# A quarter of the second tokens' expert products on GpSimd and ScalarE, value sums in PSUM, a second tile read early

## What is computed

```python
def chunk(zc):                      # 128 tokens at a time
    ...
    expert = jnp.take_along_axis(cand_idx, top_pos, axis=-1)
    gate = jax.nn.softmax(top_s, axis=-1)
    u = jnp.take(peer_u, expert, axis=0)
    act = jax.nn.gelu(jnp.einsum('chkd,cd->chk', u, zc))
    v = jnp.take(peer_v, expert, axis=0)
    w = (gate * act.astype(jnp.float32)).astype(zc.dtype)
    return jnp.einsum('chk,chkd->cd', w, v).astype(zc.dtype)
...
return rmsnorm_2(h, norm_f_g)
```

## Time and profile before

| | us |
|---|---|
| runs before (3) | 2689.12, 2693.78, 2695.74; median 2693.78 |
| profiled execution, its own time | 2692.59 |
| its span in the trace | 2690.8 |
| gather of both tables up to the last product | about 1453 to 2239 |
| pause | about 2242 to 2300 |
| dense stage | about 2300 to 2679 |

### The profile page before, as it was taken

The page is one execution under the profiler, slowest core; times in us unless marked ns, Lnnn a source line. Parts: engine busy times, 40 slices in busy tenths (PEclk is TensorE's granted clock), DMA queues, the critical chain, the costliest instruction groups (busy, mean ns, idle before and its releaser), DMA issues.

```text
span 2690.8 us, 32133 instructions
## 1 busy us (share of the span) xinstructions
PE 2288.9 (85%) x11532; PEld 1824.2 (68%) x11532; DVE 2130.7 (79%) x3227; ACT 1024.4 (38%) x1517; POOL 636.3 (24%) x706
## 2 busy tenths in 40 slices
PE   8999989999999999989899955545656558999998
PEld 7997778888888888879788831111223225777776
DVE  6986647665666566577766999899999998999997
ACT  5433554443444344454542111000234334544443
POOL 1000000000000000000002354433444442577772
PEclk9999999999999999999999975666677777999999
DMA  6533345555555555544658999999999995999996
GB/s 225 186 122 106 121 145 172 187 187 187 188 187 187 187 186 177 181 128 141 203 179 360 421 419 419 420 419 419 417 411 405 407 413 212 339 388 392 391 395 235
DMA packets 314375, 730.99 MB, mean 272 GB/s; under 512 B 21025, under 2 KB 223009, under 8 KB 275745
## 3 DMA queue, kind: packets, MB, share of 16 engines
q0 software_dynamic: 73728, 402.69, 37.0%
q1 hardware_dynamic: 240402, 325.99, 35.9%
q10 hardware_dynamic: 144, 1.05, 0.1%
HBM read 727.57 MB, written 2.10 MB: 271 GB/s over the span
## 4 chain that ended last, share of the span: by engine, by line
DVE 29%; PE 15%; DMA 8%; issue 5%; POOL 1%; ACT 1%; DVEq 0%; PEldq 0%; ACTq 0%; SPq 0%; POOLq 0%
DVE row L2483 13%; DMA row<-in_peer_u,expert 7%; DVE acc L2494 6%; PE pl L849 4%; PE pl L856 3%; PE pg L1278 2%; DVE spread_lo L2633 2%; DVE hot_b L2520 1%; PE pl L852 1%; PE pl L853 1%; PE pl L1243 1%; DMA row<-in_peer_v_rows,expert 1%; PE pl L1172 1%; POOL row L787 1%; PE pl L1269 1%
## 5 line engine op out<-in xcount | busy, mean ns | idle before, releaser
L1936 DVE TENSOR_TENSOR wlo<-raw,whi 128x1024 fp32r<-128x1024 f32 (+1 forms) x436 | 517.8, 1208 | 374.9 <-ACT whi L1335 373.1
L1243 PE MATMUL pl<-row,diag 128*128 128x512 f32 x452 | 347.0, 913 | 307.2 <-DMA row<-in_peer_v_rows,expert 268.9
L2483 DVE CUSTOM_DVE_ANT_0 row<-row,pg 128x2048 f32<-128x2048 f32 x256 | 574.4, 2283 | 35.5 <-DMA row<-in_peer_u,expert 34.5
L1335 ACT ACTIVATE whi<-raw 128x1024 fp32r<-128x1024 f32 (+1 forms) x436 | 444.1, 1038 | 412.6 <-PE pl L856 407.8
L849 PE MATMUL pl<-x_split,whi 128*128 128x512 f32 x1888 | 478.5, 395 | 10.3 <-DVE x_split L1944 5.4
L1243 PEld LDWEIGHTS pl<-row,diag 128*128 128x128 f32 x452 | 110.4, 269 | 499.6 <-issue 424.1
L787 POOL DMA_INDIRECT row<-in_peer_v_rows,expert x256 | 364.9, 1425 | 248.7 <-DVE acc L2494 88.5
L849 PEld LDWEIGHTS pl<-x_split,whi 128*128 128x128 f32 x1888 | 341.6, 190 | 74.5 <-issue 7.5
L856 PE MATMUL pl<-x_split,wlo 128*128 128x256 f32 x2656 | 373.7, 284 | 3.9 <-DVE wlo L1936 3.9
L856 PEld LDWEIGHTS pl<-x_split,wlo 128*128 128x128 f32 x2656 | 359.0, 192 | 23.1 <-DVE wlo L1936 4.5
L787 POOL DMA_INDIRECT row<-in_peer_u,expert x256 | 240.2, 938 | 364.6 <-DVE dots L2483 187.0
(11 more groups left out here) (345 smaller groups left out, 2876.3 us busy)
## 6 DMA issues: line engine op xcount, KB each, us to landing
v_tile<-in_peer_v_dense SPq DMA_DIRECT2D x128, 512.0 KB, 5.9
raw<-in_w_in SPq DMA_DIRECT2D x51, 1024.0 KB, 5.2
raw<-in_w_gate SPq DMA_DIRECT2D x44, 1024.0 KB, 5.1
raw<-in_w_up SPq DMA_DIRECT2D x44, 1024.0 KB, 5.1
raw<-in_w_out SPq DMA_DIRECT2D x32, 1024.0 KB, 5.7
raw<-in_w_down SPq DMA_DIRECT2D x32, 1024.0 KB, 5.7
wq<-in_peer_wq SPq DMA_DIRECT2D x15, 1024.0 KB, 11.7
raw<-in_w_down SPq DMA_DIRECT2D x16, 768.0 KB, 4.8
```

Source lines behind the costliest of these rows:

```text
L1243: last = mm(pl_all[:, c:c + width], diag[:, (at - 1) % 4, :], row[b][:, c - DENSE:c - DENSE + width], start=at == 1, stop=at == ADDED_ROWS ...
L1335: return nc.scalar.activation(o, i, ACT.Copy)
L1936: V.tensor_tensor(wlo[:, n % 4, 0:k, :], w[:, :, f, :], whi[:, n % 4, 0:k, :].bitcast(F32), ALU.subtract)\
L2483: V.tensor_tensor_reduce(row[b][:], row[b][:], z_tok[:], 1.0, 0.0, ALU.mult, ALU.add, dots[:, at:at + 1])\
```

## The change

- In the second tokens the products with k % 4 == 1, 32 of 128, have the user "split": GpSimd multiplies the row in place with `z_copy`, a copy of z in SBUF (VectorE writes it once, in the place of `gain_d`), after issuing the row six entries later; ScalarE sums it into `dots` ahead of the entry three later. The buffer is free after ScalarE's sum.
- One value row more is added by TensorE (114).
- Sums of value rows go to PSUM: those of the first tokens onto TensorE's sum in pl[2] and pl[3], those of the second tokens into pl[0] and pl[1], and are added to `acc` once a token set. The groups of the pause use pg[0] to pg[2].
- The second tile has a home of its own and is read in the pause (`m == 2`).
- The gains are spread in four steps at tiles 100, 102, 106 and 108, and ScalarE copies them to SBUF.

Lines that only name semaphores or stand unchanged are left out:

```diff
@@ -62,7 +62,7 @@
 DENSE = 1024
 GATHERED = D - DENSE
 EARLY = 100
-ADDED_ROWS = 113
+ADDED_ROWS = 114
...
 def row_user(table, t, n, k):
 
     if table == "u":
-        return "dot"
+        return "split" if t and k % 4 == 1 else "dot"
...
-GAIN_AT = 64
+SHARED = PH * TOPK // 4
+
+
+def dots_by(heads):
+
+    return [sum(row_user("u", *divmod(n, PH), k) == user for n in range(heads) for k in range(TOPK)) for user in ("dot", "split")]
+
+
+def shared_row(j, after):
+
+
+    return [r for r, what in enumerate(ROW_ORDER) if row_user(*what) == "split" and min(r + after, LATER + 3) == j]
+
+
+GAIN_AT = 80
+GAIN_TILES = (100, 102, 106, 108)
...
+        z_copy = sb("z_copy", "arena", TT * D + 2 * PH * NKEY, [P, D])
...
-        tile_homes = [("arena", 2 * D), ("arena", 4 * D), ("arena", 4 * D + DENSE),
-                      ("rest", choice_at), ("rest", choice_at + DENSE)]
-        high_homes = [("arena", 2 * D + DENSE), ("arena", 3 * D + DENSE), ("rest", choice_at + 2 * DENSE)]
+        tile_homes = [("arena", 2 * D), ("arena", 3 * D + DENSE), ("arena", 4 * D), ("arena", 4 * D + DENSE),
+                      ("rest", choice_at)]
+        high_homes = [("arena", 2 * D + DENSE), ("rest", choice_at + DENSE), ("rest", choice_at + 2 * DENSE)]
...
+        gain_all = sb("gain_all", "raw", 3 * D, [P, D])
...
-        used_by = {"dot": dot_done, "add": row_added, "sum": row_summed}
+        shared_done, SHARED_DONE = lam_exp, 1
+        shared_ready, SHARED_READY = sq_added, 6 * len(ADDED)
+        used_by = {"split": shared_done, "dot": dot_done, "add": row_added, "sum": row_summed}
...
-            sp.wait_ge(dot_done, PRODUCTS)
+            sp.wait_ge(dot_done, PRODUCTS - SHARED)
+            sp.wait_ge(shared_done, SHARED_DONE + SHARED)
             sp.wait_ge(row_added, EARLY)
             for m in range(NKEY):
-                if m == 1:
+                if m == 2:
...
+            def shared_product(r):
+
+                b, use, count, _ = ROW_PLAN[r]
+                if count == 1:
+                    pool.wait_ge(z_ready, 3)
+                pool.wait_ge(row_full[b], 16 * use)
+                nc.gpsimd.tensor_tensor(row[b][:], row[b][:], z_copy[:], ALU.mult).then_inc(shared_ready, 1)
...
+                if j == LATER + 4:
+                    pool.wait_ge(shared_ready, SHARED_READY + SHARED)
...
-                    pool.wait_ge(used_by[user], count)
+                    pool.wait_ge(used_by[user], count + (SHARED_DONE if user == "split" else 0))
                 at = t * HROWS + n * TOPK + k
                 dst, rows = (row[b][:], A["peer_u_2"][0]) if table == "u" else (row[b][:, 0:GATHERED], A["peer_v_rows"])
                 nc.gpsimd.indirect_dma_start(dst, None, rows, bass.IndirectOffsetOnAxis(ap=expert[:, at:at + 1], axis=0))\
                     .then_inc(row_full[b], 16)
+                for r in shared_row(j, 6):
+                    shared_product(r)
...
-                banks = [pl[0], pl[1], pg[0]] if t else [pl[0], pl[1]]
+                banks = pg[0:3] if t else pl[0:2]
...
-            def gain_rows():
+            def gain_rows(q):
 
                 pe.wait_ge(gain_in, 16)
                 pe.wait_ge(sums_ready, 1)
-                for q in range(4):
-                    last = mm(pl[q], ones[0:1, :], gain_row[0:1, q * 512:(q + 1) * 512], start=True, stop=True)
-                last.then_inc(gain_ready, 1)
+                if q >= 2:
+                    pe.wait_ge(gain_copied, 1 + q - 1)
+                mm(pl[2 + q % 2], ones[0:1, :], gain_row[0:1, q * 512:(q + 1) * 512], start=True, stop=True).then_inc(gain_ready, 1)
 
 
             pe.wait_ge(sc_ready, 2 * PH)
@@ -1321,8 +1352,8 @@
             pe.wait_ge(spread_ready, TT * GROUPS)
             for m in range(NKEY):
                 dense(m)
-                if m == NKEY - 16:
-                    gain_rows()
+                if m in GAIN_TILES:
+                    gain_rows(GAIN_TILES.index(m))
...
-                act.wait_ge(dot_done, (pair + 1) * 2 * TOPK)
+                done, shared = dots_by(2 * pair + 2)
+                act.wait_ge(dot_done, done)
+                if shared:
+                    act.wait_ge(shared_done, SHARED_DONE + shared)
...
-                bank = [pl[0], pl[1], pg[0]][g % 3] if t else pl[g % 2]
+                bank = pg[g % 3] if t else pl[g % 2]
...
+            def shared_sum(r):
+
+                b, _, count, _ = ROW_PLAN[r]
+                _, t, n, k = ROW_ORDER[r]
+                at = t * HROWS + n * TOPK + k
+                act.wait_ge(shared_ready, SHARED_READY + count)
+                activation(row[b][:], row[b][:], ACT.Copy, accum_out=dots[:, at:at + 1]).then_inc(shared_done, 1)
+
             u = 0
-            for table, t, n, k in ROW_ORDER[:LATER]:
+            for j, (table, t, n, k) in enumerate(ROW_ORDER[:LATER + 4]):
+                for r in shared_row(j, 3):
+                    shared_sum(r)
+                if j >= LATER:
+                    continue
...
+                if m - HIGHS in GAIN_TILES:
+                    q = GAIN_TILES.index(m - HIGHS)
+                    act.wait_ge(gain_ready, q + 1)
+                    copy(gain_all[:, q * 512:(q + 1) * 512], pl[2 + q % 2]).then_inc(gain_copied, 1)
+            act.wait_ge(sums_ready, 2)
             square(1, slice(DENSE, D), 43)
...
+                if t == 0 and at == ADDED_ROWS:
+                    dve.wait_ge(row_added, ADDED_ROWS)
                 if count > 1:
                     dve.wait_ge(row_summed, count - 1)
+                a = pl_all[:, 0:GATHERED] if t else pl_all[:, DENSE:]
+                if (t, n, k) == (1, 0, 0):
+                    V.tensor_scalar(a, row[b][:, 0:GATHERED], dots[:, at:at + 1], None, ALU.mult).then_inc(row_summed, 1)
+                else:
+                    V.scalar_tensor_tensor(a, row[b][:, 0:GATHERED], dots[:, at:at + 1], a, ALU.mult, ALU.add).then_inc(row_summed, 1)
+
+            def add_sums(t):
+
+                dve.wait_ge(row_summed, SUMMED_ROWS if t else HROWS - ADDED_ROWS)
                 a = acc[:, t, DENSE:]
-                V.scalar_tensor_tensor(a, row[b][:, 0:GATHERED], dots[:, at:at + 1], a, ALU.mult, ALU.add).then_inc(row_summed, 1)
-
-            def add_sums():
-
-                dve.wait_ge(row_added, ADDED_ROWS)
-                dve.wait_ge(row_summed, HROWS - ADDED_ROWS)
-                a = acc[:, 0, DENSE:]
-                V.tensor_tensor(a, a, pl_all[:, DENSE:], ALU.add).then_inc(sums_ready, 1)
+                V.tensor_tensor(a, a, pl_all[:, 0:GATHERED] if t else pl_all[:, DENSE:], ALU.add).then_inc(sums_ready, 1)
...
-                dve.wait_ge(gain_ready, 1)
+                dve.wait_ge(gain_copied, 5)
                 dve.wait_ge(fin_rstd, t + 1)
                 for q in range(4):
                     c = slice(q * 512, (q + 1) * 512)
-                    V.scalar_tensor_tensor(acc[:, t, c], acc[:, t, c], small[:, 36 + t:37 + t], pl_all[:, c], ALU.mult, ALU.mult)\
+                    V.scalar_tensor_tensor(acc[:, t, c], acc[:, t, c], small[:, 36 + t:37 + t], gain_all[:, c], ALU.mult, ALU.mult)\
...
+                    V.scalar_tensor_tensor(z_copy[:], acc[:, 1, :], small[:, 57:58], gain_d[:], ALU.mult, ALU.mult)\
+                        .then_inc(z_ready, 1)
                 for k in range(TOPK):
-                    product(t, n, k)
+                    if row_user("u", t, n, k) == "dot":
+                        product(t, n, k)
...
-                        add_sums()
+                        add_sums(0)
                 r = rows_by(m)
-            dve.wait_ge(row_summed, SUMMED_ROWS)
+            add_sums(1)
```

More of the change, by code:

```diff
@@ L395, in build @@
         freq_read = sem("freq_read")
+        gain_copied = freq_read
         par_in = sem("par_in")
@@ L1883, in _ @@
                     square(0, slice(DENSE, D), 41)
-            act.wait_ge(row_summed, SUMMED_ROWS)
+                if m - HIGHS in GAIN_TILES:
[3 more added lines that the diff above has]
+            act.wait_ge(sums_ready, 2)
             square(1, slice(DENSE, D), 43)
```

## The result

The changed kernel takes **2716.6 us** (median of 4 runs, 2714.6 to 2722.5) against 2693.3 before on the same chip: ratio 1.0088, 95% interval 1.0075 to 1.0101. The forecast was 2690 with a range to 2711; the result lies outside it. The profiled execution took 2714.57 us, its span is 2712.7.

The account below looks back on a forecast made before the run. The prediction took transfers and VectorE to stand side by side in the second tokens' gather, with 6.8 us recoverable. Terms -3.4 + 1.7 - 1.3 - 2.5 + 1.8 = -3.7 gave 2688.9, by the median 2690; range 2682 to 2711.

Parts of the forecast that it names:

- VectorE simply ceases to be the pace: Second tokens' gather: with 70.7 us of products removed, VectorE no longer limits; only 6.8 us can come back.
- term of -3.4 us for the gather: Second tokens' gather: half of the 6.8 us comes back, as only six or seven rows stay under way; ends 0 and -6.8.
- Locks between the two: Rival, 8%: in the second tokens' gather GpSimd's multiplies hold VectorE's hot-key groups and selection, 49 us; about 2707.
- 367, which still fits: Under the locks rival, VectorE's work in the second tokens' gather, 386 - 70.7 + 2.4 + 49, against some 394 us.
- Ceiling of the relief, 6.8 us: Second tokens' gather: 300 us at 410 GB/s would take 293.2 at 419.5, the most that sparing VectorE returns.
- The multiply, 4.6 us: Second tokens' gather: GpSimd's 128x2048 multiply takes 4.6 us, kept range 4.3 to 5.2, from a 128x512 add.
- GpSimd's pace as the bound: Rival, 22%: from z to the turn GpSimd's rounds set the time; 2700 to 2712 us, middle 2705.
- This stall is covered: GpSimd's first multiply waits for z_copy until about 1847.9, while eight rows (17 us) are under way.
- 2.3 us of lag is free: End of the gather: the split rows' weights are ready at 2239.7, before TensorE comes at 2242.0.
- The second tile, -2.5: Second tile read in the pause: VectorE waits less before tile 1's split, -2.5 us, ends 0 and -3.5.
- The 14th row, +1.7 and -1.3: One more row added by TensorE lengthens the pause by 1.7 us and takes 1.3 us from the dense stage.
- The sums in PSUM, +1.8: Dense stage: 142 sums each cost 13 ns more in PSUM, +1.8 us; lower end 0, +11 without overlap.

Follow-up runs that it names:

- e1: The changed kernel without the split, all 128 products of the second tokens on VectorE again; 2686.1 us, 0.9982 of the kernel before.
- e4: The changed kernel with the first tokens' hot_b reading key numbers from PSUM in place of SBUF; 2691.4 us, 0.9993 of the kernel before.
- e3: The kernel before with 32 products of the second tokens taken over 64 columns in place of 2048; 2688.8 us, ratio 0.9996.
- e10: The changed kernel without the split and with 113 added rows as before; 0.9986 of the kernel before.
- e6: The changed kernel with hot_b's key numbers in PSUM and the first head's products not split (28 rows split); 2691.2 us, 1.0000 of the kernel before.
- e8: The changed kernel with each GpSimd multiply cut in four of 128x512, no waits between; 2731.5 us, 1.0146 of the kernel before.
- e9: The changed kernel with each GpSimd multiply cut in four pieces, each waiting for the one before; 2712.5 us, 1.0084 of the kernel before.
- e7: The changed kernel without the split, with 32 GpSimd fills of a 128x2048 buffer at the multiplies' places; 2695.7 us, 1.0020 of the kernel before.

## Why the prediction was wrong

In the forecast's own sum the step that failed is "VectorE simply ceases to be the pace", with its term of -3.4 us for the gather. VectorE stayed 98% busy, with 82.5 us of held operations in the place of the products taken off, and the gather became 31.0 us longer. The forecast had this case among its rivals: **it is the rival "Locks between the two"**, at 8% the second smallest. It had the right pair of engines, and its price was too low. It counted 56 places, a chance of 38% and 2.3 us each: 49 us. Measured: 25 meetings of 3.3 us, 82.5 us. A mean over a random start underrates it, since both engines act on the same event: GpSimd comes to its multiply when VectorE frees a buffer, and VectorE's next work after that product is often the group. (That is argued from the timeline, not shown by a run.) The kind of operation was also named too narrowly: the rival speaks of two SBUF inputs, which the gate product has (9.8 of the 82.5 us), while hot_b (53.9), the conversion (15.4) and the shift (3.4) read one tile. Then it set the result against VectorE's whole stretch, "367, which still fits"; with 82.5 us in the place of 49 its own sum gives 400, which doesn't fit into its 394. And the stretch isn't even. Cut at z + 60 us and at turn - 70 us, the middle part reads:

```profile
1903.65:2174.50 270.85, 152.36 (x377) 76.43 (x378) 267.42 (x515) 98.48 (x219) 114.64 (x122) 0.74 1.01 410
```

in e1, and

```profile
1899.99:2200.54 300.55, 160.24 (x383) 79.67 (x384) 294.97 (x475) 143.69 (x267) 217.25 (x149) 0.70 0.95 380
```

in the change: VectorE is 98.7% and 98.1% busy. In e1 the transfers stand beside it at 410 GB/s; in the change they have fallen to 380, and VectorE's work alone is the length. By the groups of these windows it lost 44 us of products (85 to 65) and got 69 more of held operations (hot_b 34.2 to 84.1, conversion 1.1 to 12.3, gate product 0.6 to 8.5): +25 of the +27.6. The other products were spared at the edges, where VectorE waits for rows anyway.

**The reason given against that rival was no evidence.** "No row here shows a VectorE operation held by GpSimd" was true because GpSimd ran nothing but issues in this stretch; it says nothing of what a multiply does. The Trainium skill says in "SBUF — State Buffer", Who interferes with whom, that whichever comes first keeps the shared pair for the whole instruction, and that a conversion or TENSOR_SCALAR between SBUF tiles, and, against a GpSimd instruction that reads SBUF, an operation with two SBUF inputs are kinds that can want it. The kinds agree here: the held ones are these, the products and the reductions are not held, and one operand moved to PSUM ends it (796 to 402 ns). On who comes first the trace doesn't agree as recorded: the gate product of e4 above is recorded 0.45 us ahead of the multiply (2047.99 and 2048.44) and is held to its end all the same. Whether GpSimd's hold begins ahead of its recorded start stays open.

Point by point:
- **Ceiling of the relief, 6.8 us; term -3.4.** The ceiling holds, and the term was too large: e3 gives 0 (-0.4 us in the stretch).
- **The multiply, 4.6 us:** 4.52. **ScalarE's sum, at most 2.1:** 1.91 and 0.19 for the accumulator. GpSimd's pace as the bound (22%): false; e4 runs at its full load within 5 us of e1.
- **"This stall is covered"**, the first multiply: wrong. The eight rows under way were counted from the wait's end at 1847.9, but GpSimd had begun to wait at 1829.3, right after its last issue. It is 20.2 us without an issue, against 17 us of rows, and costs 0 to 4 us.
- **The end, "2.3 us of lag is free":** GpSimd's last three multiplies (2237.2, 2247.9, 2259.8), the issues between them and ScalarE's sum behind the last one (2264.3) are the chain to the turn; nothing of the lag was free.
- **The second tile, -2.5:** right. VectorE waits 2.6 us less for v_lo of tile 1; e10's pause part is 2.8 us shorter.
- **The 14th row, +1.7 and -1.3:** 0.5 and -1.2.
- **The sums in PSUM, +1.8:** wrong in size. A sum takes 1287 ns in place of 1282 and 1.19 us start to start where it took 1.20: nothing. GpSimd's issue in this stage fell, as forecast, from 1813 to about 1550 ns, and saved nothing. The dense part of e10 is 2.2 us shorter than before. By the spacing of its tiles this is the gain rows: before, all four products at tile 112 push the tiles behind it (4.39, 2.90, 3.11 us where 2.67 is usual), some 2 us more than the four spread ones do. I had not counted a gain there, and no run separates it.

Had the 8% been weighed by the rule and by the wait of GpSimd already visible, 1813 ns against 936, this rival would have been the forecast, and even its price of 2707 would have been 10 us short.

## What to carry to other kernels

Before work goes to GpSimd, list what VectorE does meanwhile by where its operands lie, and count every conversion, TENSOR_SCALAR and two-tile operation in SBUF as held for the rest of a GpSimd multiply between SBUF tiles (25 of 32 multiplies held one here, for 3.3 us on average); an operand in PSUM freed hot_b, the one kind on which it was tried. Then ask what the relief is worth where the work lands: cut the spared work to a stub and time it, which here would have said "nothing" before any of the split was written. With hot_b free the split still gained nothing: e4 and e6 stand at 0.9993 and 1.0000, e1 without it at 0.9982. A long instruction where a short one was is a wait that no list of waits shows.

## What the runs showed of the hardware that I had not expected

- Four GpSimd instructions that follow each other without a wait hold VectorE as one: they span 4.93 us in e8, and the longest hot_b took 5.53. A wait between them lets in one VectorE instruction per gap (e9).
- A fill, which reads nothing, holds a TENSOR_SCALAR between SBUF tiles (584 against 369 ns on average). In the meeting shown, the group would have ended at 2078.7, before the fill's recorded start at 2078.86: the hold had begun with the issue ahead of it, or the fill starts earlier than the record has it.
- Reading the key numbers from PSUM costs hot_b 33 ns (402 against 369 ns).
- Two engines held at once seem to cost more than either: GpSimd's 4.5 us pauses with hot_b free left 408 GB/s (e4), and 12 us of held time beside pauses of 1.8 us made the stretch 9 us longer (e7). The change's stretch is 30 us longer than e1's, while VectorE's busy time in it rose by 17. No run separates the two.
